# Two feed-forward networks on one Trainium2 core: gate and up products taken block by block, and a second pair of split weights

## The chip, the cores and the metric

One core of a Trainium2 chip runs one launch of the program. The metric is the time of an execution on the device in microseconds (us); less is better. The engines are TensorE (PE, products), VectorE (DVE), ScalarE (ACT), GpSimd (POOL) and SyncE (SP, which only issues transfers here). Each runs its own list of instructions in order, and semaphores hold them together.

## The reference

One layer of a decoder, for a prompt of 16 + 512 tokens and a sample group of 8 x 4 tokens, with shared weights. Only the two feed-forward networks at its ends, and the normalizations around them, matter here:

```python
D_MODEL, D_FF = 1024, 2816
def _swiglu(x, wg, wu, wd):
    return (jax.nn.silu(x @ wg) * (x @ wu)) @ wd
def _macaron_layer(x, mixer, f1g, f1u, f1d, ln1g, ln1b, ln2g, ln2b, f2g, f2u, f2d, ln3g, ln3b):
    x = _layernorm(ALPHA * x + 0.5 * _swiglu(x, f1g, f1u, f1d), ln1g, ln1b)
    m, st = mixer(x)                       # sparse attention and retention
    x = _layernorm(ALPHA * x + m, ln2g, ln2b)
    x = _layernorm(ALPHA * x + 0.5 * _swiglu(x, f2g, f2u, f2d), ln3g, ln3b)
    return x, st
```

## The kernel before

Everything is kept transposed: features on the 128 partitions, tokens along the free axis. `x` is 8 blocks (`KT`) of 128 features by 560 tokens; in the second network, `ffn(1)`, the 16 meta tokens are dropped and 544 are left. The tokens are taken in two halves of 280 or 272 columns, one PSUM bank each. The hidden layer has 22 tiles (`FT`) of 128 rows; a tile needs a gate block and an up block of weights, each 128 x 1024.

Products are made in a rounded float format, three for one: each operand is split into a high part (rounded, by ACT: `weight_high`, `x_high`) and a low part (the rest, by DVE: `weight_low`, `x_low`; for half 1 of the second network by POOL), and PE adds high x high, high x low and low x high (`wide_split`). So a tile is 2 weight blocks x 2 halves x 8 blocks of `x` x 3 = 96 products.

Weights come by SP into a ring of four slots, `wring`: slots 0 and 1 hold the gate and up block of an even tile, 2 and 3 those of an odd tile. The split parts have only one buffer for gate and one for up (`w_high`, `w_low`, two halves each): a tile's gate can be split when PE has done the last product with the gate of the tile before (semaphore `w_free0` or `w_free2`), its up block after the up block (`w_free1`, `w_free3`). `wh_done` counts high parts, `wl_done` low parts, `xl_done` blocks of `x_low`. In the loop `hidden(f, j)` on ACT splits the weights of the next tile and then takes SiLU of the present one, with a copy for the high part of the result; DVE multiplies by up and makes the low parts.

In the first network PE takes tile 0 half by half: half 0 with gate over all eight blocks of `x` (waiting for each), half 0 with up, then half 1 with gate and with up; then `tile(1)`. In the second, where the normalization `norm(1)` delivers the `x` blocks of half 0 first and of half 1 later, PE takes half 0 of tile 0 block by block with gate and up in turn, then half 1 likewise, then `tile(1)`. Tile 0's weights of the second network are split inside `norm(1)` on ACT and in the loop over the output projection on DVE. `norm` on ACT squares seven blocks (`square`), POOL adds the squares up, PE sums over the partitions with a matrix `mean`, and DVE and ACT scale.

At the start ACT's queue issues four transfers of `x` and one of the constants (`cst`, first needed near the end of the first network), SP's queue the list of pages and the four first weight blocks.

The buffer `dring` behind `z` holds pages of keys and values during the mixer; the low parts of the hidden tiles from tile 11 on lie there in the networks.

Of the kernel before, what the change touches and what calls it, by code (L numbers as in the profile page):

```python
# [15 lines left out]
ALU = mybir.AluOpType  # L16
# [73 lines left out]
def build(nc, x_t, wg1, wu1, wd1, wg2, wu2, wd2, w_in, w_out, k_pool, v_pool, i_pool, state, pages,  # L90
          consts, rope_tab, ret_tab, acc_tab, y_o, k_o, v_o, i_o, rp_o, rs_o):
    wgs, wus, wds = [wg1, wg2], [wu1, wu2], [wd1, wd2]
    with ExitStack() as ctx:
# [33 lines left out]
        w_high, w_low = over("w_high", 2048, scr_at + 2 * T * 4), over("w_low", 2048, lg_at + KT * T * 4)  # L127

# [35 lines left out]
        wh, wl = (w[:, :].rearrange("p (s n) -> p s n", s=2) for w in (w_high, w_low))  # L164
# [115 lines left out]
        def _(sp):  # L280
# [89 lines left out]
        def _(pe):  # L370
# [22 lines left out]
            def wide_split(m, p, s, high, low, k0=0, kn=KT, total=KT, parts=(0, 1), ready=None, ks=None):  # L393

                for a in parts:
                    for k in ks or range(kn):
                        if ready is not None:
                            pe.wait_ge(sem("xl_done"), ready + k + 1)
                        for j, (w_, x_) in enumerate(((wh, high), (wh, low), (wl, high))):
# [507 lines left out]
        def _(act):  # L907
# [4 lines left out]
            act.dma_start(cst[:, :], consts).then_inc(sem("cst_in"), 16)  # L912

# [3 lines left out]
            def weight_high(s, to, n=1024):  # L917

                act.wait_ge(w_in_t[s].sem, w_in_t[s].up(16))
                ev(wh[:, to, 0:n], w4[:, s, 0:n]).then_inc(sem("wh_done"), 1)  # L920

            def ffn(m):
# [22 lines left out]
                with loop(act, FT // 2 - 1, [(w, 1) for w in frees] + [(w, 16) for w in w_in_t] + [(hdone, 2)]) as i:  # L945
                    hidden(i * 2, 0)
                    hidden(i * 2 + 1, 1)
# [62 lines left out]
            weight_high(1, 1)  # L1010
# [172 lines left out]
        def _(dve):  # L1183
# [16 lines left out]
            def weight_low(s, to, n=1024):  # L1200

                dve.wait_ge(wh_done.sem, wh_done.up())
                v.tensor_tensor(wl[:, to, 0:n], w4[:, s, 0:n], wh[:, to, 0:n].bitcast(F32), ALU.subtract) \  # L1203
                    .then_inc(sem("wl_done"), 1)

            def x_lows():
                for k in range(KT):
                    dve.wait_ge(sem("xh_done"), k + 1)
                    v.tensor_tensor(xl[:, k, :], x[:, k, :], xh[:, k, :].bitcast(F32), ALU.subtract) \  # L1209
                        .then_inc(sem("xl_done"), 1)  # L1210

            def ffn(m):
                if m == 0:
                    weight_low(0, 0)
                    x_lows()
                    weight_low(1, 1)
# [22 lines left out]
                with loop(dve, FT // 2 - 1, [(sd, 2), (wh_done, 4), (hd, 2)]) as i:  # L1239
                    hidden(i * 2, 0)  # L1240
                    hidden(i * 2 + 1, 1)
# [379 lines left out]
            seq(v.scalar_tensor_tensor(halves(r7), pair(2, 1), -KT / CENTRE[1], halves(x[:, KT - 1, live(1)]), ALU.mult, ALU.add))  # L1621
# [208 lines left out]
```

## Time and profile before

| what | value |
|---|---|
| median of 3 runs | 1435.36 us (1432.1 to 1439.06) |
| profiled execution | 1438.75 us |
| its span, first to last instruction | 1437.1 us |
| PE busy | 1372.3 us, 95% of the span |
| DVE, ACT, POOL busy | 552.1, 451.1, 184.6 us |
| mean granted TensorE clock | 0.975 of full speed |

The sum of a change is made against the span and the profiled execution's own time, which lies 1.65 us above it. Busy shares are means over the whole program; the first network runs from about 9 to 430 us, the mixer to about 990, the second network from 1003 on.

### The profile page before, as it was taken

Reading aid. Unit: us, or ns where it says so; the run is one execution under the profiler, and the core shown is the slowest. Engines: PE = TensorE matmul, PEld = TensorE weight load, DVE = VectorE, ACT = ScalarE, POOL = GpSimd, SP = SyncE. Lnnn points to the kernel's source line nnn. Section 1 sums busy time; section 2 is a strip of 40 time slices with the busy share of each in tenths; the row PEclk is TensorE's granted clock in tenths of the full one; section 3 lists DMA queues with packets and bytes.
Section 4 is the critical chain, followed back from the end, with each engine's and each line's share of the span. In section 5 each row is a group of like instructions: output and inputs, shape, how many; then the busy total and the mean of one; then the engine's idle time right before and its main releaser. Section 6 shows DMA issues by size and latency. Waiting matters only on the chain.

```text
span 1437.1 us, 26868 instructions
## 1 busy us (share of the span) xinstructions
PE 1372.3 (95%) x10066; PEld 1201.4 (84%) x10066; DVE 552.1 (38%) x1105; ACT 451.1 (31%) x694; POOL 184.6 (13%) x250
## 2 busy tenths in 40 slices
PE   6999999999999999999999989998899999999994
PEld 6999999999997656777766665567799999999994
DVE  3333233322234236899020444436433333332236
ACT  3343333322233231112231403324533333322234
POOL 0000000033422301222460030003100000000020
PEclk9999999999999989999999978999899999999997
DMA  4222222233322324788757666501132222223231
GB/s 173 88 88 82 80 86 88 84 89 106 106 78 97 120 66 143 260 268 259 265 191 224 222 217 217 191 16 44 44 88 88 88 88 88 88 70 88 88 92 63
DMA packets 69454, 176.78 MB, mean 123 GB/s; under 512 B 9681, under 2 KB 13778, under 8 KB 69138
## 3 DMA queue, kind: packets, MB, share of 16 engines
q1 hardware_dynamic: 59090, 148.09, 32.5%
q0 software_dynamic: 9440, 24.18, 5.1%
q10 hardware_dynamic: 864, 3.73, 0.7%
q8 instruction: 35, 0.57, 0.2%
q14 instruction: 25, 0.20, 0.0%
HBM read 168.93 MB, written 7.02 MB: 122 GB/s over the span
## 4 chain that ended last, share of the span: by engine, by line
PE 93%; DVE 3%; ACT 2%; DMA 1%; issue 1%; ACTq 0%; POOL 0%; DVEq 0%
PE ps L377 91%; PE ps L380 2%; DMA xbuf<-in_x_t 1%; ACT scr L915 1%; DVE scr L1293 1%; DVE rbuf L1286 0%; ACT xbuf L915 0%; ACT x_high L915 0%; DVE rbuf L1298 0%; DVE w_low L1203 0%; ACT big L915 0%; ACT lg L915 0%; ACT w_high L915 0%; DVE big L1286 0%; DVE scr L1276 0%
## 5 line engine op out<-in xcount | busy, mean ns | idle before, releaser
L377 PE MATMUL ps<-x_high,w_high 128*128 128x280 f32 (+1 forms) x1408 | 414.4, 294 | 23.8 <-DVE x_low L1209 10.3
L377 PE MATMUL ps<-x_high,w_low 128*128 128x280 f32 (+1 forms) x1408 | 412.3, 293 | 0.0
L377 PE MATMUL ps<-x_low,w_high 128*128 128x280 f32 (+1 forms) x1408 | 412.1, 293 | 0.0
L1203 DVE TENSOR_TENSOR w_low<-wring,w_high 128x1024 fp32r<-128x1024 f32 (+1 forms) x136 | 166.8, 1228 | 497.2 <-ACT w_high L915 497.1
L377 PEld LDWEIGHTS ps<-x_high,w_high 128*128 128x128 f32 x1408 | 269.2, 191 | 26.6 <-issue 20.0
L915 ACT ACTIVATE w_high<-wring 128x1024 fp32r<-128x1024 f32 (+1 forms) x136 | 140.5, 1034 | 413.1 <-PE ps L377 399.3
L377 PEld LDWEIGHTS ps<-x_low,w_high 128*128 128x128 f32 x1408 | 269.9, 192 | 0.0
L377 PEld LDWEIGHTS ps<-x_high,w_low 128*128 128x128 f32 x1408 | 269.3, 191 | 0.0
L377 PE MATMUL ps<-xbuf,wring 128*128 128x280 f32 x1056 | 263.6, 405 | 5.0 <-ACT xbuf L915 4.1
L377 PEld LDWEIGHTS ps<-xbuf,wring 128*128 128x128 f32 x1056 | 197.5, 191 | 59.6 <-issue 9.1
L377 PE MATMUL ps<-h_high,w_high 128*128 128x280 f32 (+1 forms) x704 | 204.5, 290 | 0.0
L377 PE MATMUL ps<-h_high,w_low 128*128 128x280 f32 (+1 forms) x704 | 203.8, 289 | 0.0
L377 PE MATMUL ps<-h_low,w_high 128*128 128x280 f32 (+1 forms) x704 | 203.6, 289 | 0.0
L377 PEld LDWEIGHTS ps<-h_low,w_high 128*128 128x128 f32 x704 | 132.3, 188 | 0.2
L377 PEld LDWEIGHTS ps<-h_high,w_high 128*128 128x128 f32 x704 | 132.3, 188 | 0.2
L377 PEld LDWEIGHTS ps<-h_high,w_low 128*128 128x128 f32 x704 | 132.3, 188 | 0.0
L915 ACT ACTIVATE big<-ps 128x560 f32<-128x560 f32 (+2 forms) x37 | 23.4, 633 | 214.5 <-PE ps L377 210.9
L915 ACT ACTIVATE scr<-ps 128x560 f32<-128x560 f32 (+11 forms) x140 | 70.4, 523 | 58.4 <-PE ps L380 31.3
L915 ACT ACT_TABLE_LOAD x48 | 61.6, 1283 | 58.4 <-PE ps L377 54.3
L274 POOL DMA_DIRECT2D lg<-in_i_pool x64 | 33.2, 519 | 347.0 <-issue 347.0
L254 POOL DMA_DIRECT2D dring<-in_k_pool x64 | 35.1, 549 | 174.0 <-PE ps L377 167.5
L1226 DVE TENSOR_TENSOR h_low<-scr,h_high 128x560 f32 (+3 forms) x44 | 32.3, 734 | 41.8 <-ACT h_high L915 41.8
(201 smaller groups left out, 1175.3 us busy)
## 6 DMA issues: line engine op xcount, KB each, us to landing
dring<-in_v_pool SPq DMA_DIRECT2D x128, 256.0 KB, 3.5
wring<-in_wg SPq DMA_DIRECT2D x44, 512.0 KB, 3.5
wring<-in_wu SPq DMA_DIRECT2D x44, 512.0 KB, 3.5
wring<-in_w_in SPq DMA_DIRECT2D x33, 512.0 KB, 4.1
wring<-in_wd SPq DMA_DIRECT2D x32, 512.0 KB, 3.6
dring<-in_k_pool POOLq DMA_DIRECT2D x64, 256.0 KB, 4.4
dring<-in_k_pool SPq DMA_DIRECT2D x64, 256.0 KB, 3.8
wring<-in_wd SPq DMA_DIRECT2D x16, 384.0 KB, 3.1
```

The lines of the kernel that those rows point to most:

```text
L254: eng.dma_start(kv[:, s0 + b4, :], pool[bass.ds(pg, 1)].rearrange("a p n -> (a p) n")) \
L274: eng.dma_start(kis[pr // 2][64 * b2:64 * b2 + 64, pr % 2, bass.ds(i * (4 * PAGE) + j * PAGE, PAGE)], i_pool[bass.ds(pg, 1)].rearrange("a ...
L377: return nc.tensor.matmul(out, lhs, rhs, start=start, stop=stop, **kw)
L380: return nc.tensor.transpose(out, in_, ident[k0:k1, k0:k1])
L915: return nc.scalar.activation(out, in_, func, **kw)
L1203: v.tensor_tensor(wl[:, to, 0:n], w4[:, s, 0:n], wh[:, to, 0:n].bitcast(F32), ALU.subtract) \
L1226: v.tensor_tensor(row(hl, f, m), s_buf[:, j, live(m)], row(hh, f, m).bitcast(F32), ALU.subtract) \
L1293: v.reciprocal(rstd[:, cols(a, m)], rstd[:, cols(a, m)]).then_inc(own.sem, 1)
```

## The change

In the first network PE takes each block of `x` with gate and up and both halves before it goes on to the next. In the second, the weights of tile 1 are split ahead too, into a second pair of buffers (`w_high2`, `w_low2`) that lies in `dring`, and PE takes each block of half 0 with gate and up of tiles 0 and 1; half 1 follows, tile by tile. ACT's and DVE's share of the first two tiles moves out of the loop into `first_pair`, where tile 2's weights are split after tile 0's activation. At the start, weight slots 2 and 3 are loaded only when all of `x` has landed, the second weight block is split after the first block of `x`, and the constants are loaded after the splitting of `x`.

```diff
+        w_high2, w_low2 = (over(f"w_{n}2", 2048, h_at + (ZT * T + 2048 * i) * 4) for i, n in enumerate(("high", "low")))
...
             def ffn_loads(m):
                 for s in range(4):
                     f, up = divmod(s, 2)
+                    if m == 0 and s == 2:
+                        for q in range(4):
+                            sp.wait_ge(sem(f"xw_in{q}"), 16)
                     weight(s, (wus if up else wgs)[m][f], first=(m == 0))
...
-                for a in range(2 if m else 0):
-                    if a == 0:
-                        pe.wait_ge(sem("wl_done"), wl_done.up(2))
+                if m == 0:
                     for k in range(KT):
-                        pe.wait_ge(sem("xl_done"), KT * (1 + a) + k + 1)
+                        pe.wait_ge(sem("xl_done"), k + 1)
                         for up in range(2):
-                            last = wide_split(1, 2 * up, up, xh, xl, parts=(a,), ks=(k,))
-                            if a and k == KT - 1:
+                            if k == 0:
+                                pe.wait_ge(sem("wl_done"), wl_done.up())
+                            last = wide_split(0, 2 * up, up, xh, xl, ks=(k,))
+                            if k == KT - 1:
                                 last.then_inc(sem(f"w_free{up}"), 1)
-                for a in range(0 if m else 2):
-                    for up in range(2):
-                        if a == 0:
-                            pe.wait_ge(sem("wl_done"), wl_done.up())
-                        last = wide_split(m, 2 * up, up, xh, xl, parts=(a,),
-                                          ready=None if up or a > m else KT * (m + a))
-                        if a:
-                            last.then_inc(sem(f"w_free{up}"), 1)
-                tile(1)
+                    tile(1)
+                else:
+                    pe.wait_ge(sem("h_done"), hdone.up())
+                    pe.wait_ge(sem("wl_done"), wl_done.up(4))
+                    split = [dict(), dict(hi=wh2, lo=wl2)]
+                    for k in range(KT):
+                        pe.wait_ge(sem("xl_done"), KT + k + 1)
+                        for j in range(2):
+                            for up in range(2):
+                                wide_split(1, 2 * up + j, up, xh, xl, parts=(0,), ks=(k,), **split[j])
+                    for j in range(2):
+                        for up in range(2):
+                            for k in range(KT):
+                                if j == up == 0:
+                                    pe.wait_ge(sem("xl_done"), 2 * KT + k + 1)
+                                last = wide_split(1, 2 * up + j, up, xh, xl, parts=(1,), ks=(k,), **split[j])
+                            last.then_inc(sem(f"w_free{2 * j + up}"), 1)
...
-            act.dma_start(cst[:, :], consts).then_inc(sem("cst_in"), 16)
...
+                def first_pair():
+
+                    for j in range(2):
+                        for up in range(2):
+                            w = frees[2 * j + up]
+                            act.wait_ge(w.sem, w.up())
+                        ev(halves(s_buf[:, j, live(m)]), pair(j, m), ACT.Silu).then_inc(sem("s_done"), 1)
+                        act.wait_ge(hdone.sem, hdone.up())
+                        ev(hh[:, j, live(m)], s_buf[:, j, live(m)]).then_inc(sem("hh_done"), 1)
+                        if j == 0:
+                            for up in range(2):
+                                weight_high(up, up)
+
+                if m:
+                    first_pair()
...
                     for d in range(KT - 1):
                         square(1, d)
+                        if d == 3:
+                            weight_high(2, 0, out=wh2)
+                            weight_high(3, 1, out=wh2)
...
                 ev(xh[:, k, :], x[:, k, :]).then_inc(sem("xh_done"), 1)
-            weight_high(1, 1)
+                if k == 0:
+                    weight_high(1, 1)
+            act.dma_start(cst[:, :], consts).then_inc(sem("cst_in"), 16)
...
+            weight_low(2, 0, out=wl2, high=wh2)
+            weight_low(3, 1, out=wl2, high=wh2)
             for a in range(2):
                 dve.wait_ge(sem("wo_done" if a else "half_full"), 4 if a else 2)
```

PE around half 1 of the second network. Names with 53 and 54 are the old split buffers, those with 55 and 56 the new pair; `[waits ...]` names semaphores. Before, the last block of half 1, with six products to a wait, and the first product of tile 1 behind it:

```order
L377 MATMUL ps<-x_high_51,w_high_53 128x272 [waits xl_done]
L377 MATMUL ps<-x_low_52,w_high_53 128x272
L377 MATMUL ps<-x_high_51,w_low_54 128x272
L377 MATMUL ps<-x_high_51,w_high_53 128x272
L377 MATMUL ps<-x_low_52,w_high_53 128x272
L377 MATMUL ps<-x_high_51,w_low_54 128x272
L377 MATMUL ps<-x_high_51,w_high_53 128x272 [waits wl_done,h_done]
```

After the change, the end of half 0 and the first block of half 1 read so:

```order
L381 MATMUL ps<-x_high_51,w_high2_55 128x272
L381 MATMUL ps<-x_low_52,w_high2_55 128x272
L381 MATMUL ps<-x_high_51,w_low2_56 128x272
L381 MATMUL ps<-x_high_51,w_high_53 128x272 [waits xl_done]
L381 MATMUL ps<-x_low_52,w_high_53 128x272
L381 MATMUL ps<-x_high_51,w_low_54 128x272
L381 MATMUL ps<-x_high_51,w_high_53 128x272 [waits xl_done]
```

The wait for tile 1's weights is gone from behind half 1, half 0 ends with products of the new pair, and three products of half 1 follow each wait for a block of `x` instead of six.

DVE at the end of the output projection, where `big` is the sum that is normalized; before:

```order
L1266 SCALAR_TENSOR_TENSOR big<-ps,big 128x544 [waits r_done,mean_full]
L1621 SCALAR_TENSOR_TENSOR big<-ps,xbuf 128x544
L1625 TENSOR_TENSOR big<-big,ps 128x272 [waits half_full,dve_own]
L1625 TENSOR_TENSOR big<-big,ps 128x272 [waits wo_done]
L1276 TENSOR_TENSOR scr<-ps,scr 128x272 [waits shift_sq,var_full,r_done,c_done]
```

and after:

```order
L1310 SCALAR_TENSOR_TENSOR big<-ps,big 128x544 [waits r_done,mean_full]
L1665 SCALAR_TENSOR_TENSOR big<-ps,xbuf 128x544
L1231 TENSOR_TENSOR w_low2_56<-wring,w_high2_55 128x1024 [waits wh_done,dve_own]
L1231 TENSOR_TENSOR w_low2_56<-wring,w_high2_55 128x1024 [waits wh_done]
L1671 TENSOR_TENSOR big<-big,ps 128x272 [waits half_full]
L1671 TENSOR_TENSOR big<-big,ps 128x272 [waits wo_done]
L1320 TENSOR_TENSOR scr<-ps,scr 128x272 [waits shift_sq,var_full,r_done,c_done]
```

Two splits stand ahead of the two halves of the last block.

ACT behind the normalization, after the change; the last row of the normalization stands first:

```order
L923 ACTIVATE xbuf<-big,cst 128x272
L923 ACT_TABLE_LOAD [waits w_free1,w_free0]
L923 ACTIVATE scr<-ps 128x544 [waits kvi_out]
L923 ACTIVATE h_high<-scr 128x544 [waits h_done]
L923 ACTIVATE w_high<-wring 128x1024 [waits w_in0]
L923 ACTIVATE w_high<-wring 128x1024 [waits w_in1]
L923 ACTIVATE scr<-ps 128x544 [waits w_free3,w_free2]
```

Before, a table load and `w_high` for slots 2 and 3 stood first here, ahead of a second table load and the SiLU (`scr<-ps`); now the SiLU of tile 0 comes first and then the weights of tile 2, in slots 0 and 1.

## Rows read from the trace of the kernel before

**Rows 1.** The page's part 4: shares of the chain that ended last, by engine.
```profile
PE 93%; DVE 3%; ACT 2%; DMA 1%; issue 1%; ACTq 0%; POOL 0%; DVEq 0%
```
**Rows 2.** Waits of PE in the whole span: total us, times, longest.
```profile
PE ps L377 <- DVE x_low L1209: 10.3, 2, 9.4
...
PE ps L377 <- DVE w_low L1203: 4.5, 3, 3.5
...
PE ps L377 <- POOL x_low L1699: 3.4, 1, 3.4
```
**Rows 3.** Timeline of PE, first network: start, duration, operation, [idle before].
```profile
9.43 0.57 PE L377 MATMUL ps<-x_high,w_high 128*128 128x280 f32 x1 [9.43 <-DVE x_low L1209]
...
28.49 0.29 PE L377 MATMUL ps<-x_high,w_low 128*128 128x280 f32 x1
29.54 0.37 PE L377 MATMUL ps<-x_high,w_high 128*128 128x280 f32 x1 [0.77 <-DVE w_low L1203]
```
**Rows 4.** Timeline of ACT, first network, between its first two tiles.
```profile
25.79 1.28 ACT L915 ACT_TABLE_LOAD   x1 [9.90 <-PE ps L377]
27.08 1.06 ACT L915 ACTIVATE w_high<-wring 128x1024 fp32r<-128x1024 f32 x1
```
**Rows 5.** Timeline of DVE, first network.
```profile
8.55 2.69 DVE L1209 TENSOR_TENSOR x_low<-xbuf,x_high 128x560 fp32r<-128x560 f32 x4
...
28.17 1.22 DVE L1203 TENSOR_TENSOR w_low<-wring,w_high 128x1024 fp32r<-128x1024 f32 x1 [11.02 <-ACT w_high L915]
```
**Rows 6.** Timeline of PE, beginning of the second network.
```profile
1003.15 0.57 PE L377 MATMUL ps<-x_high,w_high 128*128 128x272 f32 x1 [5.59 <-DVE x_low L1281]
...
1015.04 0.59 PE L377 MATMUL ps<-x_high,w_high 128*128 128x272 f32 x1 [3.38 <-POOL x_low L1699]
...
1023.59 0.28 PE L377 MATMUL ps<-x_high,w_low 128*128 128x272 f32 x1
1027.36 0.36 PE L377 MATMUL ps<-x_high,w_high 128*128 128x272 f32 x1 [3.49 <-DVE w_low L1203]
```
**Rows 7.** The chain in order of time, whole span: start, us, what.
```profile
1027.36 389.37 PE ps L377 x3084
```
**Rows 8.** Stretches: length, busy us of PE, PEld, DVE, ACT, POOL, granted clock, DMA.
```profile
1003.10:1008.00 4.90, 4.85 (x21) 4.88 (x22) 4.31 (x12) 4.90 (x11) 0.00 (x0) 0.50 0.00 0
...
1018.30:1023.90 5.60, 5.57 (x36) 4.52 (x34) 1.75 (x4) 3.79 (x8) 3.35 (x4) 0.99 0.00 0
...
1028.60:1031.90 3.30, 3.30 (x18) 3.30 (x17) 1.45 (x2) 0.89 (x2) 0.00 (x0) 0.51 0.00 0
```
**Rows 9.** Timeline of POOL, low parts of half 1 of the second network.
```profile
1018.72 1.03 POOL L1699 TENSOR_TENSOR x_low<-xbuf,x_high 128x272 fp32r<-128x272 f32 x1 [0.61 <-ACT xbuf L915]
...
1022.02 0.77 POOL L1699 TENSOR_TENSOR x_low<-xbuf,x_high 128x272 fp32r<-128x272 f32 x1 [0.24 <-ACT xbuf L915]
```
**Rows 10.** Timeline of ACT, SiLU and high part of tile 0, second network.
```profile
1028.21 0.62 ACT L915 ACTIVATE scr<-ps 128x544 f32<-128x544 f32 x1
1029.73 0.66 ACT L915 ACTIVATE h_high<-scr 128x544 f32 x1 [0.89 <-DVE scr L1223]
```
**Rows 11.** Timelines of SP, ACT, POOL and PE, output projection and normalization 1.
```profile
976.50 0.33 SPq L287 DMA_DIRECT2D wring<-in_wu  x1
...
984.80 1.20 ACT L915 ACTIVATE acc<-big 128x544 f32<-128x544 f32 x2 [1.57 <-POOL scr L1651]
...
985.53 7.29 POOL L1651 TENSOR_TENSOR scr<-scr,acc 128x544 f32<-128x544 f32 x5 [0.83 <-ACT acc L915]
...
994.64 1.08 PE L377 MATMUL ps<-scr,cst 128*128 128x272 f32 x4
```
**Rows 12.** Timeline of DVE, output projection.
```profile
977.15 3.49 DVE L1203 TENSOR_TENSOR w_low<-wring,w_high 128x1024 fp32r<-128x1024 f32 x2
...
990.64 0.44 DVE L1625 TENSOR_TENSOR big<-big,ps 128x272 f32<-128x272 f32 x1
```
**Rows 13.** Transfers issued from 1.5 to 2.0 us: queue, count, KB, us to landing.
```profile
wring<-in_wu SPq DMA_DIRECT2D x1, 512.0 KB, 7.2
```

More of the change, by code:

```diff
@@ L163, in build @@
         xh, xl, hh, hl = tiles(x_high, KT), tiles(x_low, KT), tiles(h_high, FT), tiles(h_low, FT)
-        wh, wl = (w[:, :].rearrange("p (s n) -> p s n", s=2) for w in (w_high, w_low))
+        wh, wl, wh2, wl2 = (w[:, :].rearrange("p (s n) -> p s n", s=2) for w in (w_high, w_low, w_high2, w_low2))
         w4 = wring[:, :].rearrange("p (s n) -> p s n", s=4)
@@ L391, in weight, with wide_split @@
                 pe.wait_ge(w_in_t[s].sem, w_in_t[s].up(16))
-            def wide_split(m, p, s, high, low, k0=0, kn=KT, total=KT, parts=(0, 1), ready=None, ks=None):
+            def wide_split(m, p, s, high, low, k0=0, kn=KT, total=KT, parts=(0, 1), ks=None, hi=wh, lo=wl):
                 for a in parts:
                     for k in ks or range(kn):
-                        if ready is not None:
-                            pe.wait_ge(sem("xl_done"), ready + k + 1)
-                        for j, (w_, x_) in enumerate(((wh, high), (wh, low), (wl, high))):
+                        for j, (w_, x_) in enumerate(((hi, high), (hi, low), (lo, high))):
                             last = mm(ps[:, 2 * p + a, 0:HW[m]], w_[:, s, k * P:(k + 1) * P],
@@ L911, in _, with weight_high @@
                               .rearrange("p (k t) -> p k t", k=2)).then_inc(sem(f"xw_in{q}"), 16)
-            act.dma_start(cst[:, :], consts).then_inc(sem("cst_in"), 16)
             def ev(out, in_, func=ACT.Copy, **kw):
                 return nc.scalar.activation(out, in_, func, **kw)
-            def weight_high(s, to, n=1024):
+            def weight_high(s, to, n=1024, out=wh):
                 act.wait_ge(w_in_t[s].sem, w_in_t[s].up(16))
-                ev(wh[:, to, 0:n], w4[:, s, 0:n]).then_inc(sem("wh_done"), 1)
+                ev(out[:, to, 0:n], w4[:, s, 0:n]).then_inc(sem("wh_done"), 1)
             def ffn(m):
@@ L944, in ffn @@
                 hdone = Tally(sem("h_done"), 2 + FT * m)
-                with loop(act, FT // 2 - 1, [(w, 1) for w in frees] + [(w, 16) for w in w_in_t] + [(hdone, 2)]) as i:
-                    hidden(i * 2, 0)
-                    hidden(i * 2 + 1, 1)
+                def first_pair():
[11 more added lines that the diff above has]
+                    first_pair()
+                with loop(act, FT // 2 - 1 - m, [(w, 1) for w in frees] + [(w, 16) for w in w_in_t] + [(hdone, 2)]) as i:
+                    hidden(i * 2 + 2 * m, 0)
+                    hidden(i * 2 + 2 * m + 1, 1)
                 hidden(FT - 2, 0)
@@ L1198, in _, with weight_low @@
             wh_done = Tally(sem("wh_done"))
-            def weight_low(s, to, n=1024):
+            def weight_low(s, to, n=1024, out=wl, high=wh):
                 dve.wait_ge(wh_done.sem, wh_done.up())
-                v.tensor_tensor(wl[:, to, 0:n], w4[:, s, 0:n], wh[:, to, 0:n].bitcast(F32), ALU.subtract) \
+                v.tensor_tensor(out[:, to, 0:n], w4[:, s, 0:n], high[:, to, 0:n].bitcast(F32), ALU.subtract) \
                     .then_inc(sem("wl_done"), 1)
@@ L1210, in x_lows @@
                         .then_inc(sem("xl_done"), 1)
+                    if k == 0:
+                        weight_low(1, 1)
             def ffn(m):
@@ L1237, in output, with first_pair @@
                                            ALU.mult, ALU.add).then_inc(sem("r_done"), 1)
-                with loop(dve, FT // 2 - 1, [(sd, 2), (wh_done, 4), (hd, 2)]) as i:
-                    hidden(i * 2, 0)
-                    hidden(i * 2 + 1, 1)
+                def first_pair():
+                    for j in range(2):
+                        dve.wait_ge(sd.sem, sd.up())
+                        v.tensor_tensor(halves(s_buf[:, j, live(m)]), halves(s_buf[:, j, live(m)]), pair(2 + j, m), ALU.mult) \
+                            .then_inc(sem("h_done"), 1)
+                        dve.wait_ge(hd.sem, hd.up())
+                        v.tensor_tensor(hl[:, j, live(m)], s_buf[:, j, live(m)], hh[:, j, live(m)].bitcast(F32), ALU.subtract) \
+                            .then_inc(sem("hl_done"), 1)
+                        if j == 0:
+                            for up in range(2):
+                                weight_low(up, up)
+                if m:
+                    first_pair()
+                with loop(dve, FT // 2 - 1 - m, [(sd, 2), (wh_done, 4), (hd, 2)]) as i:
+                    hidden(i * 2 + 2 * m, 0)
+                    hidden(i * 2 + 2 * m + 1, 1)
                 hidden(FT - 2, 0)
```

1 line of the change is left out of this document (removed).

## Prediction

> **What bounds the kernel now.** I read the page's chain first, then the waits of TensorE (PE), then the order of time around the places where the two networks begin. The chain that ended last is 93% PE [rows 1], so a microsecond counts only if PE stands still in it or runs at its lower clock. The reader is to see how short the list of waits at the change's places is [rows 2]: 10.3 us for the first network's `x_low` on VectorE (DVE; 9.4 of them before the first product, so 0.9 later), and for the second network 3.4 for `x_low` on GpSimd (POOL) and, out of 4.5 for `w_low`, one wait of 3.5. Removable idle time is therefore 3.4 + 3.5 us at the second network and about 0.9 + 1.0 at the first; what the lower clock costs comes on top. A product at full clock takes 389.37 / 3084 = 0.1263 us in the chain behind the second network's first tiles [rows 7]; at the lower clock 21 products take 4.85 us, 0.23 each [rows 8].
>
> **Second network, before.** PE starts tile 0 at 1003.15, runs dry, starts again at 1015.04, issues its last product at 1023.59, and starts tile 1 at 1027.36 [rows 6]. The last wait is this: tile 1's weights can be split only into the buffer that tile 0 has just left, behind a table load on ScalarE (ACT). The row of 1028.6 to 1031.9 shows a granted clock of 0.51, the 1.2 GHz level [rows 8], right after that pause: 3.3 us at half rate, 1.65 us lost. Tile 2 so starts at 1027.36 + 96 x 0.1263 + 1.65 = 1041.1.
>
> **Second network, after.** All four weight blocks are split during the normalization, and PE has 96 products for half 0 instead of 48. It starts at 1003.15 as before, if the normalization isn't delayed (below). From 1003.1 to 1008.0 the clock is 0.50 and 21 products start [rows 8]; I keep that stretch. The other 75 take 9.5 us, so half 0 ends near 1017.5. Its supply isn't short: a block of `x` now feeds 12 products, 1.5 to 2.7 us, where before it fed 6. Half 1 then meets POOL, whose last four `x_low` start between 1018.72 and 1022.02, the last taking 0.77 [rows 9]: block 7 is there at 1022.8. Tile 0's gate takes only 3 products (0.38 us) of each block there and waits for blocks 4 to 7; it ends at 1022.8 + 0.1 + 0.4 = 1023.3. From there 72 products need no more `x`: 9.1 us, the end at 1032.4.
>
> What is late next are the weights of tile 2. They are split behind tile 0's activation: the release comes when PE is done with tile 0's up block, 24 products on (1026.3, plus about 0.3 until an engine acts on it), then the table load, 1.28 (as at the start [rows 4]), from the SiLU's start to the end of its high part 1029.73 + 0.66 - 1028.21 = 2.18 [rows 10], a `w_high` 1.06 [rows 4], a `w_low` 1.22 [rows 5], and 0.14 until PE moves. The sum is 1026.6 + 5.9 = 1032.5. PE waits 0.1 us at most. Tile 2 starts at 1032.5 instead of 1041.1: **8.6 us less**. That is more than 3.4 + 3.5, since 1.65 of the low clock go too, and less than all of it, since the paced blocks give some back.
>
> On this table load the Trainium skill, ScalarE: Activation LUTs, section What ACT_TABLE_LOAD costs, names a drain of about 1.38 us beside the 1.28 of the load for each switch of sets. This trace disagrees: the load starts at 25.79 and `w_high` at 27.08, 1.29 later [rows 4]. By the page tile 2 would start 1.38 us later and the gain be 7.2; the sum goes by the row.
>
> **What is inserted in the normalization.** ACT gets two `w_high` (1.06 each) after square 3, the second of the two in 1.20 us from 984.80 [rows 11], so at 986.0; square 4 then starts near 988.1. Its reader on POOL is the third of five additions that take 7.29 us without a gap from 985.53 [rows 11], 1.46 each: it started at 988.45 and starts at 988.8. The sum of squares is ready at about 993.2 instead of 992.8, and PE reads it at 994.64 [rows 11]: hidden, by 1.4 us. DVE gets two `w_low` ahead of the first half of the last block, which stands at 990.64 [rows 12]. They cost 2 x 1.22 alone, or 3.49 as the pair at 977.15 [rows 12], where POOL's additions ran beside it. I take the dearer, since POOL adds until 993: done at 994.1, the half at 994.5. Its readers on PE come after the products at 994.64, four of 0.23 us, so at 995.56 or later. Hidden, with 1 us left; without that cover the dearer price is 3.5 us. The other bound is 0. The copies of weights themselves are the ones that the loop did before, moved, and so are their loads; the loop's loads change nothing but their start.
>
> **First network.** The order changes the same way, but without the second buffer. Before: products start at 9.43, tile 0's last one at 28.49 (over at 28.8), tile 1's first at 29.54, 0.8 us idle [rows 3]. After: `x` and two weight blocks come first. The second weight block landed 7.2 us after its issue at 1.75, so at 8.95 [rows 13]; the queues were shared and it gets no later. ACT splits it until 10.0 (1.06 [rows 4]), DVE until 11.3, then an `x_low` every 0.67 us [rows 5]. From 11.4 PE never waits, because each block is 12 products. PE starts at the low clock there: its first product takes 0.57, as at 1003.15, the last of tile 0 takes 0.29 [rows 3, 6]. I keep 3.3 to 5 us at that clock, the two low stretches of [rows 8]: by 14.7 to 16.4 some 20 to 28 of the 96 products are done, and the rest, at 0.13, ends at 24.5 to 25.2 instead of 28.8. But gate and up now end 6 products, 0.8 us, apart instead of 24 products, 3.1 us. Tile 1 still needs the release of the gate's buffer, and from ACT's table load at 25.79 to tile 1 at 29.54 [rows 3, 4] it is 3.75 us, 3.85 with the release. So tile 1 starts at 27.6 to 28.3, 1.2 to 1.9 us earlier, with 3.1 us of idle time in front of it instead of 0.8. If the clock falls after this pause as it did after 1023.59, 1.65 us go back. Bounds: -0.5 and +1.9. I take 0, near the fall, since that one came after a pause hardly longer. The constants come some 10 us later and are first read hundreds of us on: nothing.
>
> **Sum.** Span 1437.1 - 8.6 = 1428.5. The profiled execution took 1438.75, so it would take 1430.2; it was 3.4 us above the median of the runs shown, 1435.36. From the median: **1427**.
>
> **Rivals.**
> - *The clock falls in the paced blocks.* Between 1018.9 and 1022.8 PE would work 0.38 us in each 1.0. Against: from 1018.3 to 1023.9 it was already paced by the same blocks, with six products each, and the clock was 0.99 [rows 8]. For: it now works half as much there as it did. If it falls, dense work after 1023.3 starts at half rate, and the clock came back only after 3.3 to 5 us of it [rows 8]: 5 us, 2.5 us lost, gain 6.1, 1429.3; with 0.5 lost at the start, 1430. Beside it stands the Trainium skill, TensorE: Matmul & The Clock Gate, section HAM oscillation — how this bites in real kernels: bursts of matmuls with idle time between them send the clock back and are each started cold.
> - *Slower: DVE's two `w_low` hold back the normalization.* They wait for ACT, which waits for the weights of slots 2 and 3, and the last block's two halves stand behind them in DVE's queue; everything up to PE's start waits for those halves. Each us by which they end after 995 moves the whole kernel. It decides from 1003.5 on: 8.6 us. For: DVE's row shows that such a pair can stretch. Against: the later of those loads is issued at 976.50 [rows 11], 9.5 us before ACT needs it, and a load took 7.2 with four queued together [rows 13]. At 8.6 + 8 us late: 1443.
> - *The wait only moves.* Tile 2's weights come late, because the loads of slots 0 and 1 now start with tile 0's end and share the bandwidth: if `w_high` starts 6 us later than reckoned, 2.6 are left, 1432.8. Against: the release of slot 0 comes at 1023.6, and even the 7.2 us of the start [rows 13] bring it at 1030.8, 0.7 after ACT wants it.
>
> **Chances.** The forecast 0.50, the clock falling 0.34, the table load as the page has it 0.04 (1428.2), the wait only moved 0.08, slower 0.04. A measurement of this kernel tells about 0.5%, 7.2 us, from no change. The forecast lies 1.4 us beyond that line and the runs shown spread by 3.5 to either side, so I give it 0.75 for faster; the clock's fall 0.3; the others little: faster 0.50, same 0.46, slower 0.04. The range holds the first three with the bounds of the start (gain 10.5 to 5.6 us) and 3 us of spread: 1422 to 1433. The forecast's own is 1423.5 to 1430.
>
> **What would show it.** PE: no pause at 1011 or after tile 0 of the second network, pauses of 0.6 us between groups of three products at 1019 to 1023, tile 2 near 1032.5. PE's start near 1003.15 shows the normalization untouched; any delay there shows the DVE pair. A granted clock near 0.5 after 1021 is the first rival. At the start a wait for `w_low` of about 3 us before tile 1 should stand where 0.8 stood. I am wrong if the normalization's end moves by more than 1 us, or if tile 2 waits for its weights by more than 2.

## The result, and the profile after

The changed kernel took 1426.27 us in the median of 7 runs (1423.05 to 1429.18), the kernel before 1438.63 in 7 runs (1432.1 to 1439.51): ratio 0.9931, 95% interval 0.9916 to 0.9945, so 0.7% faster, 9.9 us by the ratio (7.9 to 12.1 by its interval). The two medians lie further apart, 12.4 us; what follows goes by the ratio. Forecast were 1427 us and 8.6 us less. The two profiled executions differ by more, 1438.75 and 1424.5, spans 1437.1 and 1422.8; which part of that is the change's is the first question of the experiments.

The page's chain after the change, by engine; it is PE's as before [rows 1]:

```profile
PE 93%; DVE 3%; ACT 3%; issue 1%; DMA 1%; POOL 0%; SPq 0%; ACTq 0%; DVEq 0%
```

PE's waits in the whole span after the change (total us, times, longest):

```profile
PE ps L381 <- DVE x_low L1237: 9.4, 1, 9.4
...
PE ps L381 <- DVE w_low L1231: 3.3, 2, 3.1
...
PE ps L381 <- POOL x_low L1745: 1.7, 4, 0.6
```

Against [rows 2], POOL's one wait of 3.4 became four of at most 0.6, and the `w_low` wait of 3.5 at the second network is gone. The 3.1 that is left is a new one, in the first network, where 0.77 stood [rows 3].

The second network: PE's timeline (start, duration, operation, idle before).

```profile
997.37 0.57 PE L381 MATMUL ps<-x_high,w_high 128*128 128x272 f32 x1 [5.59 <-DVE x_low L1325]
...
1012.54 0.29 PE L381 MATMUL ps<-x_high,w_low 128*128 128x272 f32 x1
1012.81 0.39 PE L381 MATMUL ps<-x_high,w_high 128*128 128x272 f32 x1
...
1014.08 0.39 PE L381 MATMUL ps<-x_high,w_high 128*128 128x272 f32 x1 [0.63 <-POOL x_low L1745]
...
1017.48 0.29 PE L381 MATMUL ps<-x_high,w_low 128*128 128x272 f32 x1
...
1026.64 0.38 PE L381 MATMUL ps<-x_high,w_high 128*128 128x272 f32 x1
```

The last row is tile 2's first product: 29.27 us after PE's start, where the forecast had 1032.5 - 1003.15 = 29.35. Before, it came 37.85 us after PE's start at 1003.15 [rows 6]:

```profile
1041.00 0.29 PE L377 MATMUL ps<-x_high,w_high 128*128 128x272 f32 x1
```

In the stretches around it (length, busy us of PE, PEld, DVE, ACT, POOL, granted clock, DMA share, GB/s) the clock is low at the start and then never again:

```profile
997.40:1001.80 4.40, 4.40 (x19) 4.40 (x20) 4.17 (x12) 4.40 (x10) 0.00 (x0) 0.50 0.00 0
1001.90:1012.70 10.80, 10.80 (x87) 10.71 (x86) 9.67 (x17) 6.66 (x13) 3.60 (x4) 1.00 0.00 0
1012.80:1017.60 4.80, 3.06 (x16) 2.17 (x16) 1.53 (x3) 3.27 (x7) 3.31 (x4) 1.00 0.02 3
1017.60:1026.60 9.00, 9.00 (x74) 8.98 (x72) 2.70 (x4) 4.46 (x5) 0.00 (x0) 1.00 0.54 163
```

ACT and DVE on the way to tile 2's weights, after the change:

```profile
1020.90 1.28 ACT L923 ACT_TABLE_LOAD   x1 [4.67 <-PE ps L381]
1022.19 0.62 ACT L923 ACTIVATE scr<-ps 128x544 f32<-128x544 f32 x1
1023.71 0.66 ACT L923 ACTIVATE h_high<-scr 128x544 fp32r<-128x544 f32 x1 [0.89 <-DVE scr L1272]
1024.27 1.99 ACT L923 ACTIVATE w_high<-wring 128x1024 fp32r<-128x1024 f32 x2
```

```profile
1025.35 2.36 DVE L1231 TENSOR_TENSOR w_low<-wring,w_high 128x1024 fp32r<-128x1024 f32 x2 [0.23 <-ACT w_high L923]
```

From table load to the end of the first `w_low`, half-way through its row, is 1020.90 to about 1026.6, 5.7 us; forecast 5.7 and then 0.14 to PE. Before, a `w_high` came straight behind the load [rows 4]; here the SiLU does, again 1.29 later.

The first network: PE, ACT and stretches.

```profile
9.41 0.57 PE L381 MATMUL ps<-x_high,w_high 128*128 128x280 f32 x1 [9.41 <-DVE x_low L1237]
11.35 0.60 PE L381 MATMUL ps<-x_high,w_high 128*128 128x280 f32 x1 [0.20 <-DVE w_low L1231]
...
24.82 0.29 PE L381 MATMUL ps<-x_high,w_low 128*128 128x280 f32 x1
28.20 0.37 PE L381 MATMUL ps<-x_high,w_high 128*128 128x280 f32 x1 [3.09 <-DVE w_low L1231]
```

```profile
24.45 1.28 ACT L923 ACT_TABLE_LOAD   x1 [10.48 <-PE ps L381]
25.74 2.00 ACT L923 ACTIVATE w_high<-wring 128x1024 fp32r<-128x1024 f32 x2
```

```profile
28.20:31.60 3.40, 3.40 (x18) 3.40 (x19) 1.89 (x3) 2.15 (x3) 0.00 (x0) 0.65 0.17 67
```

Tile 0 ends 3.7 us earlier than in [rows 3], tile 1 starts 1.34 earlier behind a pause of 3.09, and the clock falls right after it. SP's load of the ninth weight block, which tile 2's gate releases, stands at 48.74 us; before it stood at 48.56. In these two profiles the first network's part nets nothing, as forecast, by the pause and the fall that were forecast; how far that is the luck of two profiles is taken up below.

### The profile page after: what moved, and what is told of

Same layout as the page of the kernel before. It is cut to its first block, busy times and chain, and to the rows that moved or that the text cites. A ratio compares the mean times of both kernels' runs of the same rounds, so it can differ in the third digit from the quotient of the medians.

```text
span 1422.8 us, 26829 instructions
## 1 busy us (share of the span) xinstructions
PE 1361.0 (96%) x10066; PEld 1194.3 (84%) x10066; DVE 552.4 (39%) x1105; ACT 425.2 (30%) x675; POOL 185.4 (13%) x250
## 4 chain that ended last, share of the span: by engine, by line
PE 93%; DVE 3%; ACT 3%; issue 1%; DMA 1%; POOL 0%; SPq 0%; ACTq 0%; DVEq 0%
PE ps L381 91%; PE ps L384 2%; ACT scr L923 1%; DVE scr L1337 1%; ACT xbuf L923 1%; DMA wring<-in_wu 1%; DVE rbuf L1330 0%; ACT x_high L923 0%; DVE rbuf L1342 0%; DVE big L1342 0%; DVE big L1330 0%; ACT big L923 0%; ACT lg L923 0%; DVE w_low L1231 0%; ACT w_high L923 0%
## 5 line engine op out<-in xcount | busy, mean ns | idle before, releaser
L923 ACT ACTIVATE h_high<-scr 128x560 f32 (+3 forms) x44 | 29.3, 666 | 59.1 <-DVE scr L1252 57.3
```

The lines of the kernel that those rows point to most:

```text
L923: return nc.scalar.activation(out, in_, func, **kw)
```

## The experiments

Each profile was read by the same marks: the ninth weight load of the first network (a), the stretch from there to PE's first product in the second network (b), from there to the ninth weight load of the second network, the fifth after that product, released by its tile 2 (c), and the rest. In b every kernel has the same code but for the splits of tile 1's weights near its end. All from SP's and PE's timelines; the clock is that of 430 to 990 us. SP's rows for a and for the end of c, before:

```profile
48.56 0.34 SPq L287 DMA_DIRECT2D wring<-in_wg  x1
1047.47 0.34 SPq L287 DMA_DIRECT2D wring<-in_wg  x1
```

and after:

```profile
48.74 0.33 SPq L288 DMA_DIRECT2D wring<-in_wg  x1
1033.13 0.33 SPq L288 DMA_DIRECT2D wring<-in_wg  x1
```

| kernel | a | b | c | rest | clock | ratio, interval |
|---|---|---|---|---|---|---|
| before | 48.56 | 954.59 | 44.32 | 389.63 | 0.96 | |
| before again | 48.30 | 950.82 | 44.30 | 389.58 | 0.97 | one run, 1434.72 us |
| after | 48.74 | 948.63 | 35.76 | 389.67 | 0.98 | 0.9931 (0.9916 to 0.9945) |
| second network only | 48.10 | 950.86 | 35.77 | 389.57 | 0.97 | 0.9939 (0.992 to 0.9957) |
| first network only | 48.56 | 948.61 | 44.25 | 390.18 | 0.98 | 0.9992 (0.9978 to 1.0006) |
| second pair only | 47.41 | 953.72 | 39.24 | 389.63 | 0.97 | 0.9964 (0.995 to 0.9977) |
| loads only | 45.62 | 948.32 | 44.24 | 389.72 | 0.98 | one run, 1429.57 us |
| order only | 54.45 | 951.79 | 44.31 | 389.65 | 0.97 | one run, 1441.84 us |
| loads and second network | 46.43 | 949.37 | 35.71 | 389.69 | 0.98 | 0.9931 (0.9911 to 0.9952) |
| after, pair in both networks | 44.04 | 953.40 | 35.68 | 389.68 | 0.97 | 0.9918 (0.9897 to 0.9939) |
| after, half 1 by gate and up | 48.61 | 948.68 | 33.11 | 389.70 | 0.98 | 0.992 (0.9902 to 0.9938) |
| after, both of these | 43.85 | 960.15 | 33.11 | 389.69 | 0.95 | 0.9901 (0.9879 to 0.9922) |
| the same again | 42.74 | 948.88 | 33.09 | 390.19 | 0.98 | 0.9895 (0.9875 to 0.9915) |

**The second network alone.** The kernel after, with the first network's order and the loads of before:

```diff
-                    for k in range(KT):
-                        pe.wait_ge(sem("xl_done"), k + 1)
-                        for up in range(2):
...
+                    for a in range(2):
+                        for up in range(2):
+                            if a == 0:
+                                pe.wait_ge(sem("wl_done"), wl_done.up())
+                            for k in range(KT):
...
-                    if m == 0 and s == 2:
-                        for q in range(4):
-                            sp.wait_ge(sem(f"xw_in{q}"), 16)
```

> Only the second network's part of the change: products in the order of the kernel after, second pair of split weights; the first network and the loads at the start as before. Theory (all that lasts comes from the second network): from PE's first product of the second network to tile 2's first product 29.3 us, as in the kernel after, against 37.85 before; whole kernel 8.6 us faster than before, ratio 0.994. Rival one (the start brings what lies between 8.6 and the measured 9.9 us): the same 29.3 us, but a ratio of 0.995 or above here, and below 1 for the first network alone. Rival two (the mixer between the networks is shortened by the change, 5.8 us in the two profiles): from tile 2's first product of the first network to PE's start in the second 955 us, as after, and not 961, as before.

Column c is 35.77 as in the kernel after, 8.55 less than before, and the ratio 0.9939 is the forecast 0.994. Rival one is not needed, but the interval doesn't exclude 1 or 2 us for it.

**The first network alone.** The kernel before, with the first network's part:

```diff
+                for k in range(0 if m else KT):
+                    pe.wait_ge(sem("xl_done"), k + 1)
+                    for up in range(2):
+                        if k == 0:
+                            pe.wait_ge(sem("wl_done"), wl_done.up())
+                        last = wide_split(0, 2 * up, up, xh, xl, ks=(k,))
...
+                    if m == 0 and s == 2:
+                        for q in range(4):
+                            sp.wait_ge(sem(f"xw_in{q}"), 16)
```

> Only the first network's part: products block by block in its first tile, two weight loads and the constants behind x; the second network as before. Theory: tile 1 starts near 28.2 us after about 3.1 us of waiting, the clock falls behind it for 3.3 us, and nothing is left when tile 2 begins: ratio 1.000, between 0.9985 and 1.0015. Rival one (the start pays): ratio 0.998 or below, 3 us or more. Rival two (the mixer): the stretch between the networks 955 us if the first network's part is what shortens it, 961 if not.

The pause in front of tile 1 is 3.09 us, the ninth load at 48.56, the ratio 0.9992 with 1 inside its interval. The interval leaves room for 3.2 us gained or 0.9 lost, so rival one isn't excluded here either; column a shows no gain. The stretch b is 948.61, 6.0 us shorter than in the profile of before, which is what rival two expects (its 955 and 961 count from a mark some 6.3 us ahead of a); the next run bears on that.

**The kernel before again.** No edit.

> The kernel before once more, unchanged, for a second profile. Theory (the mixer's length changes from run to run with the places where the clock falls, change or not): the stretch between the networks anywhere from 954 to 962 us, the second network's first two tiles within 1.7 us of 37.85. Rival two (the mixer is shorter because of the change): 961 again, within 1 us.

Its stretch b is 950.82, 3.8 us shorter than in the first profile of the very same program, so rival two's 961 within 1 us doesn't hold. Over the thirteen profiles b runs from 948.3 to 960.2; the longest is that of a kernel with more edits, whose second profile gives 948.88. So b differs from run to run by as much as the 6.0 us of the 14.3 between the two profiled spans that lie in it, and nothing shows these 6.0 to be the change's. A smaller share is not excluded: the five profiles with the old loads have b from 950.8 to 954.6, six of the eight with the new loads 948.3 to 949.4, and the other two 953.4 and 960.2. What b does goes with the clock. The stretch of 430 to 990 us in the profile of before and in the two of the last kernel of the table, in that order:

```profile
430.00:990.00 560.00, 537.51 (x3661) 372.66 (x3660) 260.01 (x757) 146.79 (x321) 110.61 (x150) 0.96 0.55 180
```

```profile
430.00:990.00 560.00, 541.48 (x3655) 375.78 (x3656) 254.78 (x747) 146.54 (x318) 109.93 (x149) 0.95 0.55 178
```

```profile
430.00:990.00 560.00, 537.60 (x3688) 374.92 (x3686) 264.33 (x760) 151.29 (x329) 114.39 (x151) 0.98 0.55 178
```

By the trace's records of the granted clock, 41.0, 53.3 and 27.5 us of these 560 were at 0.50. Half of the time at 0.50 is lost where PE works all through, so the last two should differ by up to 12.9 us; their b differ by 11.3. Why the clock falls in one run and not in another was not tried.

**The second pair alone.** The second-network kernel with tile 0 in the order of before:

```diff
-                    for k in range(KT):
-                        pe.wait_ge(sem("xl_done"), KT + k + 1)
-                        for j in range(2):
-                            for up in range(2):
-                                wide_split(1, 2 * up + j, up, xh, xl, parts=(0,), ks=(k,), **split[j])
...
+                    for a in range(2):
+                        for k in range(KT):
+                            pe.wait_ge(sem("xl_done"), KT * (1 + a) + k + 1)
+                            for up in range(2):
+                                last = wide_split(1, 2 * up, up, xh, xl, parts=(a,), ks=(k,))
...
+                    for up in range(2):
+                        wide_split(1, 2 * up + 1, up, xh, xl, **split[1]).then_inc(sem(f"w_free{2 + up}"), 1)
```

> The second pair of split weights alone, in the second network: tile 0 in the order of before (half 0, wait, half 1), then tile 1 from the pair split ahead; first network as before. Theory (wait for w_low 3.5 us and the low clock behind it 1.65 us go, the wait of 3.4 us for half 1 stays): tile 2's first product 32.7 us after PE's start in this network, 5.1 us less than before, ratio 0.9964. Rival (the buffer is what counts and the order only moves the wait): 29.3 us, ratio 0.994. A third outcome, 35 us or more, would mean that tile 2's weights now come late.

c is 39.24, 5.08 less than before, against 5.1 forecast; the ratio 0.9964 is the one forecast. PE's wait for half 1 stays, 3.7 us in its list of waits there, and none for `w_low`:

```profile
PE ps L378 <- DVE x_low L1319: 5.6, 1, 5.6
PE ps L378 <- POOL x_low L1739: 3.7, 1, 3.7
```

So of the 8.55 us 5.1 are the second pair's, and 3.5 are what the order adds to it.

**The loads alone.** The kernel before, with weight slots 2 and 3 behind `x`, the second split after the first block and the constants later.

```diff
+                    if m == 0 and s == 2:
+                        for q in range(4):
+                            sp.wait_ge(sem(f"xw_in{q}"), 16)
...
+                if k == 0:
+                    weight_high(1, 1)
+            act.dma_start(cst[:, :], consts).then_inc(sem("cst_in"), 16)
```

> Of the first network's part only the loads and splits: two weight loads behind x, the second weight block split after the first block of x, the constants later; PE's order as before. Theory: x lands 2.6 us earlier, PE's waits of 0.9 and 0.2 us go, tile 1 starts 1 to 2 us before 29.54, its wait in front stays about 0.8 us and the clock doesn't fall there. Rival (x is not what PE waits for at the start): tile 1 within 0.3 us of 29.54.

Tile 1 starts 2.93 us earlier than before, more than the theory's 1 to 2, and the ninth load with it. PE's timeline and the stretch behind:

```profile
25.55 0.29 PE L380 MATMUL ps<-x_high,w_low 128*128 128x280 f32 x1
26.61 0.37 PE L380 MATMUL ps<-x_high,w_high 128*128 128x280 f32 x1 [0.77 <-DVE w_low L1207]
```

```profile
26.60:30.00 3.40, 3.39 (x26) 3.40 (x27) 1.96 (x2) 2.46 (x4) 0.00 (x0) 1.00 0.45 154
```

The pause is still 0.77 and the clock 1.00 behind it, where the kernel after had 3.09 and 0.65. So the loads gain and the block order gives back.

Not all of the 2.93 is the loads'. At the start PE's products follow each other every 0.23 us, later every 0.13, and that step came at 21.7 us in the profile of before and at 15.5 here. The two rows of before around it:

```profile
21.34 0.43 PE L377 MATMUL ps<-x_high,w_low 128*128 128x280 f32 x1
...
21.78 0.29 PE L377 MATMUL ps<-x_low,w_high 128*128 128x280 f32 x1
```

Four profiles have the first network of before (before, before again, second network only, second pair only). Their column a runs from 47.41 to 48.56, the smallest where PE spent the least time at the slow pace. Against these four the loads alone gained 1.8 to 2.9 us.

**The order alone.** The first network's diff above without its loads.

> The kernel before, with the first network's tile 0 taken block by block and nothing else. Theory (the order alone costs, since the pause of 3.1 us and the low clock behind it come whatever the loads do, and x lands late as before): 3.1 us of waiting in front of tile 1, the low clock behind it, the ninth weight load at 50 us or later, against 48.3 to 48.6 before. Rival (with x late, the order hides the waits for x and gains what it later loses): 48 to 49 us.

The pause is 3.09 again. The ninth load is at 54.45, 5.9 us later than before: the theory's 50 us or later holds, the rival doesn't. Most of the loss isn't the pause's: the second weight block is still split after all of `x`, and every block of `x` now needs it.

```profile
9.47 0.57 PE L377 MATMUL ps<-x_high,w_high 128*128 128x280 f32 x1 [9.47 <-DVE x_low L1209]
17.29 0.60 PE L377 MATMUL ps<-x_high,w_high 128*128 128x280 f32 x1 [6.08 <-DVE w_low L1203]
33.90 0.37 PE L377 MATMUL ps<-x_high,w_high 128*128 128x280 f32 x1 [3.09 <-DVE w_low L1203]
```

It so tells that the order needs the earlier split; of the pause's price it tells only that the pause comes whatever the loads do.

**The loads with the second network.** The kernel after with the order of before in the first network's tile 0.

```diff
-                            last = wide_split(0, 2 * up, up, xh, xl, ks=(k,))
+                                last = wide_split(0, 2 * up, up, xh, xl, parts=(a,), ks=(k,))
```

> The kernel after, with the order of products in the first network's tile 0 put back to that of before; the new loads and splits at the start and the second network's part stay. Theory (the loads gain about 3 us, the block order there gives 3 back by the pause in front of tile 1 and the low clock behind it): SP's ninth weight load, released by tile 2's gate, at 45.6 us instead of 48.7, ratio to before 0.9915, 3 us better than the change. Rival (what the loads alone gained in one look came from where the clock rose in that run): 47 to 48.5 us, ratio 0.9935.

The ninth load stands at 46.43, 2.3 us before that of the kernel after, between what the two sides expected: 0.8 from the theory's 45.6, 0.6 from the rival's 47. The rival has a part in it: the products' step from 0.23 to 0.13 us came at 17.3 us here and at 15.5 with the loads alone. And 46.43 is 1.0 to 2.1 us below the four profiles with the first network of before. The ratio, 0.9931, is no better than the change's; its interval of 2 thousandths to either side holds both expected ratios. In the profile the first network is shorter without the block order; in the time it isn't shown.

**The second pair in the first network too.** The kernel after, with tile 1's weights split ahead there and `first_pair` used in both networks:

```diff
-                    tile(1)
+                    pe.wait_ge(sem("h_done"), hdone.up())
+                    for up in range(2):
+                        pe.wait_ge(sem("wl_done"), wl_done.up())
+                        wide_split(0, 2 * up + 1, up, xh, xl, hi=wh2, lo=wl2).then_inc(sem(f"w_free{2 + up}"), 1)
...
-                if m:
-                    first_pair()
+                first_pair()
...
+            for up in range(2):
+                weight_high(2 + up, up, out=wh2)
...
```

> The kernel after, with the second pair of split weights used in the first network too: slots 2 and 3 are split ahead while PE works on tile 0, and tile 2's weights behind tile 0's activation. Theory (the 3.1 us pause in front of tile 1 and the low clock behind it, 1.6 us, cost what the earlier start had gained): tile 1 follows tile 0 without a pause, tile 2 starts 4.7 us earlier than in the kernel after, ratio to before 0.990. Rival (the pause only moves on to tile 2, whose weights now come late): tile 2 starts at most 1 us earlier than in the kernel after, ratio as after, 0.993.

PE's whole list of waits from 0 to 430 us, the last of them at 11.34:

```profile
PE ps L381 <- DVE x_low L1241: 9.4, 1, 9.4
PE ps L381 <- DVE w_low L1235: 0.2, 1, 0.2
```

The ninth load is at 44.04, 4.70 us before that of the kernel after. The pause of 3.1 and the low clock behind it, 1.6, were the price of the block order there. The ratio, 0.9918, is between the two that were expected, with b 4.8 longer in its profile than in that of the kernel after.

**Gate and up in turn for half 1.** The kernel after, in the second network:

```diff
-                        for up in range(2):
-                            for k in range(KT):
-                                if j == up == 0:
-                                    pe.wait_ge(sem("xl_done"), 2 * KT + k + 1)
+                        for k in range(KT):
+                            if j == 0:
+                                pe.wait_ge(sem("xl_done"), 2 * KT + k + 1)
+                            for up in range(2):
...
```

> The kernel after, with gate and up of tile 0 taken in turn for each block of half 1 in the second network, so six products follow each wait for a block of x and not three. Theory (PE starves at the blocks that POOL delivers every 1.0 us): the waits of 1.7 us there go, tile 2 starts about 27.6 us after PE's start in this network instead of 29.3, ratio to before 0.9925. Rival (tile 2 hangs on its weights, ready 0.1 us before PE in the kernel after): the waits go, but PE waits before tile 2, which stays at 29.3 within 0.5 us.

c is 33.11, 2.65 less. The theory's direction held, its size was short by 1 us: from 1012.54 to 1017.48 the kernel after issued 15 products in 4.94 us that take 1.9 without pauses, 3.1 lost, while the list of waits counts 1.7. A row's idle time begins where the last product's modelled 0.29 us end, though the next could start 0.125 after it, so each pause shows 0.16 too short, and the first product behind one takes 0.1 more. For the same reason the list of waits for this kernel counts none behind PE's start, though two short pauses are left:

```profile
1015.81 0.29 PE L381 MATMUL ps<-x_high,w_low 128*128 128x272 f32 x1
1016.03 0.40 PE L381 MATMUL ps<-x_high,w_high 128*128 128x272 f32 x1
...
1016.76 0.29 PE L381 MATMUL ps<-x_high,w_low 128*128 128x272 f32 x1
1017.04 0.40 PE L381 MATMUL ps<-x_high,w_high 128*128 128x272 f32 x1
```

With 0.1 more for the first product behind each they cost 0.45 us, and 3.1 less 0.45 is the gain of 2.65. Tile 2 didn't hang on its weights.

**Both together**, twice.

> The last two together on top of the kernel after: second pair in the first network, gate and up in turn for half 1 in the second. Theory: 4.7 and 1.7 us add up, 15 us less than before, ratio 0.9895. Rivals as for the two alone: 0.993.

> The kernel with the second pair in both networks and gate and up in turn for half 1 once more, beside the two above on one chip. Theory: ninth weight load at 43.9 us and 33.1 us from PE's start in the second network to its fifth weight load, as in its first profile; ratio to before 0.989, 2 to 3 us better than the kernel with the order of before in the first network. Rival (the rest of what it gains there is lost in the mixer): ratio 0.992, equal to that kernel.

Ratios 0.9901 and 0.9895; columns a and c add up as expected, 4.7 to 5.8 and 11.2 us less than in the profile of before. The second ratio is the theory's 0.989 rather than the rival's 0.992: its median lies 5.4 us below that of the kernel with the order of before in the first network, measured beside it, though their intervals still touch. This is the fastest version tried, in the median 1423.89 and 1420.92 us.

## Why the prediction was right

**Second network.** Forecast 8.6 us, measured 8.56 in column c, and it holds term by term: PE's start to tile 2 29.27 us (29.35), the low clock at the start (997.40 to 1001.80 at 0.50, 4.4 us where 4.9 were kept), four waits at POOL's blocks, a chain to tile 2's weights that ends 0.1 us ahead of PE. The pauses cost 3.1 us; the forecast had them in without naming their sum, by reckoning with the landing of POOL's last block, 19.65 us after PE's start, where it came 19.70 after by POOL's timeline (1017.07 - 997.37).

**Table load.** The SiLU starts 1.29 us after the load's start, as `w_high` did before [rows 4]. The Trainium skill, ScalarE: Activation LUTs, section What ACT_TABLE_LOAD costs, adds a drain of about 1.38 us to the load, by which it would be 2.66; this trace disagrees again.

**Normalization.** Forecast hidden, and it is: PE's start comes 8.51 us after the product that sums the squares, before 1003.15 - 994.64 [rows 6, 11], after 997.37 - 988.86. But DVE's pair cost more than the dearer bound, 4.07 us against 3.49, and the margin was less than the forecast 1 us:

```profile
984.86 4.07 DVE L1231 TENSOR_TENSOR w_low<-wring,w_high 128x1024 fp32r<-128x1024 f32 x2
988.85 0.77 DVE L1671 TENSOR_TENSOR big<-big,ps 128x272 f32<-128x272 f32 x2
```

```profile
979.75 8.09 POOL L1697 TENSOR_TENSOR scr<-scr,acc 128x544 f32<-128x544 f32 x5 [0.83 <-ACT acc L923]
...
985.71 2.13 POOL L1697 TENSOR_TENSOR scr<-scr,acc 128x544 f32<-128x544 f32 x1
```

```profile
988.86 1.08 PE L381 MATMUL ps<-scr,cst 128*128 128x272 f32 x4
989.78 0.62 PE L381 MATMUL ps<-big,cst 128*128 128x272 f32 x2
```

The halves are done at 989.27 and 989.62, and PE reads the first at 989.78, a margin of 0.5 us. POOL's additions took 8.09 instead of 7.29 [rows 11]. The forecast had put a delay there on ACT's `w_high`, 0.4 us; that didn't come, since the third addition starts 2.99 us after the first, before 2.97. The 0.8 is the fifth addition's, 2.13 us instead of 1.34, which ran while DVE split: beside each other both took longer. By these rows a third block there would have moved the network; no run tried it.

**First network.** Forecast zero, measured 48.74 against 48.56 at the ninth load; the pause 3.09 (3.1), tile 1 at 28.20 (27.6 to 28.3), the clock falling behind it. That it is a sum of two opposite terms is shown by the two kernels with the loads and without the order (45.62 and 46.43), and by the second pair, which takes the pause away. That they cancel to 0.2 us is partly luck: of the four profiles with the first network of before, that of before is the one whose clock rose last. These four have the ninth load at 47.41 to 48.56, the three with loads and order at 48.56 to 48.74, so the part costs 0 to 1.3 us by these profiles, 0.5 by their means, which is the forecast's lower bound; in the time, 0.9992, no cost is seen.

**Rivals.** The clock didn't fall in the paced blocks: from 1012.80 to 1017.60 PE was busy 3.06 of 4.80 us, and the clock was 1.00; nor in the three other profiles with this order (0.99 to 1.00 from 1003 to 1040). Where PE paused once for 3.1 it fell, and so it did in the second network before, behind the waits of 3.4 and 3.5 [rows 6]; the first of these falls:

```profile
1015.00:1018.30 3.30, 3.26 (x14) 3.26 (x15) 3.30 (x5) 2.93 (x7) 2.86 (x3) 0.50 0.00 0
```

The Trainium skill, TensorE: Matmul & The Clock Gate, section HAM oscillation — how this bites in real kernels, tells of bursts of matmuls that each start cold behind a wait of some microseconds for a transfer. The trace agrees for the single pauses of 3.1 to 3.5 us (0.50 to 0.65 behind them). The pauses between the paced blocks, at most 0.8 us from the last product's turn to the next product, are not that case, but pauses shorter than 3 us came before a fall too: in three of the four profiles with the first network of before the clock fell there behind pauses of at most 1.3 us. With the second network's part alone they were 1.21 and 0.69 us, and the two stretches read:

```profile
13.70:17.00 3.30, 1.82 (x10) 1.15 (x9) 2.26 (x3) 2.18 (x3) 0.00 (x0) 1.00 0.38 158
17.10:20.40 3.30, 2.98 (x13) 2.99 (x14) 0.26 (x1) 0.00 (x0) 0.00 (x0) 0.50 0.00 0
```

So the rival was nearer than its failure here tells. DVE's pair did not hold back the normalization, and tile 2's weights were not late.

**The total.** The ratio says 9.9 us with an interval from 7.9 to 12.1; the marks say 8.4 that belong to the change. The rest lies inside what stretch b does from run to run, and no run here shows it to be the change's. That the median came within 0.7 us of 1427 is partly luck too: the forecast was made from the median of three runs, 1435.36, and from that of the seven, 1438.63, the same 8.6 us would give 1430.0.

## What to carry to other kernels

Where a pipeline is refilled, give its first stages a second buffer and enough products for each block that arrives: here 5.1 us came from the buffer, 3.5 from the order, and 2.65 more from six products to a block instead of three. An order that hides late data can end all its weights at once and so leave the split of the next ones uncovered; look at what is released last and how far apart. Compare profiles by marks around the changed code, not by their spans, when the code between them scatters more than the change is worth.

## What the runs showed of the hardware

The middle part, nearly the same code in every kernel, took 948.3 to 960.2 us over thirteen profiles, with a granted clock of 0.95 to 0.98 in it; two profiles of one program differed by 11.3 us there. DVE's pair of splits took 2.36 us alone and 4.07 beside POOL's additions, of which the one that ran while DVE split took 2.13 instead of 1.34. Behind PE's single pauses of 3.1 to 3.5 us between dense stretches the granted clock fell to 0.50, and once behind two of 1.21 and 0.69 us; with listed pauses of at most 0.63 us between groups of three products it stayed at 1.00.
